# A two-block transformer forward pass on one core: one weight split ahead of a norm's last square, gated-attention scores ahead of their states, and row factors at the end on ScalarE and GpSimd

## The reference

```python
# first block, second norm
hffn = modulate(rmsnorm(x, g_norm2[l]), shift2, scale2)
a, u = jnp.split(jnp.einsum('bsd,df->bsf', hffn, w_ffn_in[l]), 2, axis=-1)

# second block, GLA in chunks of 64 tokens
att = jnp.where(causal, jnp.einsum('nbhtd,nbhsd->nbhts', q_in, k_in), 0.0)
o_intra = jnp.einsum('nbhts,nbhsv->nbhtv', att, vc)
def step(state, xs):
    qi, kd, vv, bl = xs
    o = jnp.einsum('bhtd,bhdv->bhtv', qi, state)
    state = state * jnp.exp(bl)[:, :, 0, :, None] + jnp.einsum('bhsd,bhsv->bhdv', kd, vv)
    return state, o

# the end
y = xf * lax.rsqrt(jnp.mean(xf * xf, axis=-1, keepdims=True) + EPS) * g
```

## Time and profile before

| | us |
|---|---|
| median of 3 runs | 1921.94 |
| lowest, highest run | 1920.91, 1922.42 |
| profiled execution, its own time | 1923.94 |
| its span | 1922.1 |
| PE busy | 1879.3 (98%) |
| DVE, ACT, POOL busy | 868.0, 687.2, 516.4 |

### The profile page before, as it was taken

One profiled execution on the slowest core, in us unless ns is written; L12 is line 12 of the kernel. 1 busy time (PEld: TensorE's weight loads), 2 busy tenths in 40 slices (PEclk: granted clock), 3 DMA queues, 4 the chain that ended last, 5 costly groups with the idle time before them and its releaser, 6 DMA issues.

```text
span 1922.1 us, 21539 instructions
## 1 busy us (share of the span) xinstructions
PE 1879.3 (98%) x8653; PEld 1463.2 (76%) x8653; DVE 868.0 (45%) x1352; ACT 687.2 (36%) x1021; POOL 516.4 (27%) x285
## 2 busy tenths in 40 slices
PE   7999999999999999989999999999999999999998
PEld 6777778878777777867888888777676778888886
DVE  6466542645261213334333333657477654423433
ACT  5555541223232323443221223425446432212223
POOL 4433334444353534410000000234345311100100
PEclk9999999999999999999999999999899999999999
DMA  9411223534443223324323322422122123222321
GB/s 302 144 46 65 66 66 132 175 121 153 132 141 100 66 88 110 102 74 118 114 82 95 108 80 77 113 88 84 58 72 73 46 99 104 93 88 89 108 88 44
DMA packets 182332, 192.47 MB, mean 100 GB/s; under 512 B 10155, under 2 KB 166065, under 8 KB 181977
## 3 DMA queue, kind: packets, MB, share of 16 engines
q1 hardware_dynamic: 179704, 180.84, 29.3%
q0 software_dynamic: 1104, 5.24, 1.0%
q10 hardware_dynamic: 1424, 5.00, 0.7%
HBM read 188.95 MB, written 4.72 MB: 101 GB/s over the span
## 4 chain that ended last, share of the span: by engine, by line
PE 87%; DVE 8%; ACT 2%; issue 2%; POOL 1%; DMA 0%; ACTq 0%; DVEq 0%; SPq 0%; POOLq 0%
PE bank L1465 23%; PE bank L1468 23%; PE bank L1466 23%; PE bank L1487 2%; PE bank L1486 2%; PE bank L1485 2%; PE bank L1561 2%; DVE left L1819 2%; PE bank L1495 1%; DVE ADA L1777 1%; PE bank L1531 1%; PE bank L1547 1%; PE bank L1511 1%; PE bank L1447 1%; PE bank L1448 1%
## 5 line engine op out<-in xcount | busy, mean ns | idle before, releaser
L2559 POOL TENSOR_TENSOR wl<-stg,wh 128x1024 fp32r<-128x1024 f32 x150 | 364.8, 2433 | 853.5 <-ACT wh L2200 853.1
L1465 PE MATMUL bank<-hH,wh 128*128 128x512 f32 x1264 | 522.6, 413 | 6.3 <-DVE hL L1933 6.0
L1468 PE MATMUL bank<-hH,wl 128*128 128x512 f32 x1264 | 502.4, 397 | 0.0
L1466 PE MATMUL bank<-hL,wh 128*128 128x512 f32 x1264 | 502.1, 397 | 0.0
L2200 ACT ACTIVATE wh<-stg 128x1024 fp32r<-128x1024 f32 (+2 forms) x292 | 298.3, 1024 | 283.6 <-PE bank L1468 202.8
L1465 PEld LDWEIGHTS bank<-hH,wh 128*128 128x128 f32 x1264 | 239.2, 189 | 78.4 <-issue 25.5
L1468 PEld LDWEIGHTS bank<-hH,wl 128*128 128x128 f32 x1264 | 238.9, 189 | 57.9
L1466 PEld LDWEIGHTS bank<-hL,wh 128*128 128x128 f32 x1264 | 239.8, 190 | 53.5 <-issue 2.9
L1759 DVE TENSOR_TENSOR wl<-stg,wh 128x1024 fp32r<-128x1024 f32 (+2 forms) x142 | 168.4, 1188 | 243.7 <-ACT wh L2200 243.2
L1465 PE MATMUL bank<-h2H,wh 128*128 128x512 f32 x352 | 140.6, 399 | 0.0
L1468 PE MATMUL bank<-h2H,wl 128*128 128x512 f32 x352 | 139.5, 396 | 0.0
(11 more groups left out here) (324 smaller groups left out, 2565.3 us busy)
## 6 DMA issues: line engine op xcount, KB each, us to landing
stg<-in_w_in SPq DMA_DIRECT2D x54, 1024.0 KB, 5.2
stg<-in_w_ffn_in SPq DMA_DIRECT2D x22, 1024.0 KB, 5.1
stg<-in_w_ada SPq DMA_DIRECT2D x16, 1024.0 KB, 5.2
stg<-in_w_ffn_gate SPq DMA_DIRECT2D x11, 1024.0 KB, 5.1
stg<-in_w_ffn_up SPq DMA_DIRECT2D x11, 1024.0 KB, 5.1
stg<-in_w_ffn_down SPq DMA_DIRECT2D x10, 1024.0 KB, 5.0
stg<-in_w_ada SPq DMA_DIRECT2D x16, 512.0 KB, 6.8
stg<-in_w_proj_ret SPq DMA_DIRECT2D x8, 1024.0 KB, 5.0
```

The costliest lines, as they stand in the source:

```text
L1465: T.matmul(ps, wh, xh, start=j["first"] and k == 0, stop=False)
L1466: T.matmul(ps, wh, xl, start=False, stop=False)
L1468: t = T.matmul(ps, wl, xh, start=False, stop=j["stop"] and last)
L2559: G.tensor_tensor(lo, src, hi, ALU.subtract).then_inc(s["w_lo_pool"], 1)
```

## The change

Three separate edits. First, the preparation of the FFN's third product stands in the last `out_job`, between the bank's release and the square, and no longer behind `a2`. Second, in the GLA the scores of a pair's first head stand ahead of the pair's states, three advances (before: one) lie between the states and `go`, and the scores of the second head stand right behind the first head's `go` step. Third, at the end DVE forms `fs/D + EPS` once per row behind the first half, ACT forms the factor alone as exp(-0.5 ln(...)) from the second half's sum, POOL scales the low half, and DVE the high half.

```diff
@@ out_job
             give(("gemm", n, 0))
+            if f == KT - 1:
+                p.prepare(p.ahead)
             sums("n2", f)
@@ norm2
         emit("a2")
-        p.prepare(p.ahead)
@@ gla
+        def scores(hd):
+            take("Z", ("gs", hd))
+            emit("gs", hd)
+            give(("gs", hd))
...
                 emit("kv", r, cc)
             yield
+            scores(2 * r)
+            yield
             emit("st", r)
             give(("kv", r, 0))
             give(("kv", r, 1))
-            yield
+            yield from rest(3)
             for hh in range(2):
                 hd = 2 * r + hh
-                take("Z", ("gs", hd))
-                emit("gs", hd)
-                give(("gs", hd))
-                yield
                 take("C", ("go", hd))
                 emit("go", hd)
                 yield
+                if hh == 0:
+                    scores(hd + 1)
                 emit("gsq", hd)
@@ sync, last_row
-                sp.wait_ge("a_end", 2 * i + 2)
+                sp.wait_ge("p_end", i + 1)
...
-                sp.wait_ge("v_end", 3 * i + 3)
+                sp.wait_ge("v_end", i + 1)
@@ vector, fin
                     V.tensor_tensor(dst, dst, GFB[:, 0:S], ALU.mult).then_inc(s["v_fin"], 1)
+                    V.tensor_scalar(fs[:, i:i + 1], fs[:, i:i + 1], 1.0 / D, EPS, ALU.mult, ALU.add).then_inc(s["v_fin"], 1)
@@ vector, last_row
-                ve.wait_ge("a_fin", 5 + i)
-                V.tensor_tensor(fd[:, i:i + 1], fs[:, i:i + 1], fs[:, 4 + i:5 + i], ALU.add).then_inc(s["v_end"], 1)
-                ve.wait_ge("a_end", 2 * i + 1)
-                V.reciprocal(fr[:, i:i + 1], fd[:, i:i + 1]).then_inc(s["v_end"], 1)
-                ve.wait_ge("v_end", 3 * i + 2)
+                ve.wait_ge("a_end", 2 * i + 2)
                 V.scalar_tensor_tensor(hi, hi, fr[:, i:i + 1], GFB[:, S:D], ALU.mult, ALU.mult).then_inc(s["v_end"], 1)
@@ scalar, fin
                     if c == 3:
-                        A_.preload_act_table(ACTF.Sqrt)
+                        A_.preload_act_table_set("natural_log_exp_and_others")
@@ scalar, last_row
-                lo = XT[:, i, 0:S]
-                ac.wait_ge("v_end", 3 * i + 1)
-                A_.activation(fd[:, i:i + 1], fd[:, i:i + 1], ACTF.Sqrt, bias=e6, scale=1.0 / D).then_inc(s["a_end"], 1)
-                ac.wait_ge("v_end", 3 * i + 2)
-                ac.wait_ge("v_fin", i + 1)
-                A_.activation(lo, lo, ACTF.Copy, scale=fr[:, i:i + 1]).then_inc(s["a_end"], 1)
+                ac.wait_ge("v_fin", 2 * i + 2)
+                ac.wait_ge("a_fin", 5 + i)
+                A_.activation(fd[:, i:i + 1], fs[:, 4 + i:5 + i], ACTF.Ln, bias=fs[:, i:i + 1], scale=1.0 / D).then_inc(s["a_end"], 1)
+                ac.wait_ge("a_end", 2 * i + 1)
+                A_.activation(fr[:, i:i + 1], fd[:, i:i + 1], ACTF.Exp, scale=-0.5).then_inc(s["a_end"], 1)
@@ gpsimd
+            def last_row(i):
+                lo = XT[:, i, 0:S]
+                po.wait_ge("a_end", 2 * i + 2)
+                G.tensor_scalar(lo, lo, fr[:, i:i + 1], None, ALU.mult).then_inc(s["p_end"], 1)
```

More of the change, by code:

```diff
@@ L1088 @@
 a_sq v_sq v_a2 v_n2 v_m1 v_x3 v_sc v_best a_gb v_gc a_gd v_gd a_ge p_gf a_gg p_gh a_gh p_gi
-kv_even v_st a_gsq a_gate p_gate v_mn p_al v_ag a_ae v_as av a_silu p_silu a_fin v_fin v_end a_end
+kv_even v_st a_gsq a_gate p_gate v_mn p_al v_ag a_ae v_as av a_silu p_silu a_fin v_fin v_end a_end p_end
 """.split()
@@ L2650, in qas @@
                     low("h4", pr, QA[:, pr, :])
+            def last_row(i):
+                lo = XT[:, i, 0:S]
+                po.wait_ge("a_end", 2 * i + 2)
+                G.tensor_scalar(lo, lo, fr[:, i:i + 1], None, ALU.mult).then_inc(s["p_end"], 1)
             mine = {"split": split, "n1": n1, "masks": masks_, "sbw": sbw, "ret_load": ret_load, "rot_sum": rot_sum, "rvv": rvv,
-                    "bias_first": bias_first, "bias_copy": bias_copy, "ffn_a": ffn_a, "gf": gf, "gh": gh, "gi": gi, "gn": gn, "lg": lg, "qas": qas}
+                    "bias_first": bias_first, "bias_copy": bias_copy, "ffn_a": ffn_a, "gf": gf, "gh": gh, "gi": gi, "gn": gn, "lg": lg, "qas": qas, "last_row": last_row}
             for name, *at in p.order:
```

## The result

The changed kernel takes 1918.65 us in the median of 15 runs (1916.75 to 1918.94), the kernel before 1921.79 us beside it (15 runs, 1920.91 to 1922.46): a ratio of 0.9981 with a 95% interval of 0.9973 to 0.9989, 3.1 us saved where 7.9 were forecast. The profiled execution of the changed kernel took 1918.94 us (span 1917.1), against 1923.94: 5.0 less. Lines of the code after the first edits stand 3 to 6 further down than before (L1465 is now L1471, L1933 is L1939, L1663 is L1669, L2077 is L2083).

A forecast was written before the change was run, and what follows sets the result against it. PE, busy 98% of the span, bounds the kernel, so time comes from its waits, low clock and the end's chain: -1.94 - 1.4 - 6.2 + 1.6 = -7.9, from 1923.9 to 1916.0, less 2.0 gives 1914.0 us; range 1911 to 1919.5.

The forecast's parts named there:

- the clock term of the second edit: GLA: the clock no longer falls, so 13.7 us of low clock at 0.455 save 6.2 us; bounds 0 and -6.8.
- First edit, -1.94: Second norm: the split moved into idle ACT and DVE time lets PE start at 857.90, not 859.84, saving 1.94 us.
- Rival D: Second norm: ACT takes the moved split no sooner and the square waits; up to 1.9 lost, 1915.9; inside the forecast's 0.62.
- I take no difference: Behind the second norm: the low clock for 4.4 us of PE's work stays as it was; bounds -2.0 and +1.0.
- rival B: Second norm: the clock does not fall there either, 2.0 less, 1912.0; chance 0.08.
- Second edit, waits, -1.4: GLA, first head: waits of 2.13 and 0.36 us give way to one of 1.1 ahead of the scores, saving 1.4 us.
- The other three heads: 0: GLA, remaining heads: the reordering changes nothing, taken as 0; bounds -0.5 to +1.5 for moved DVE waits.
- Rival A: GLA: the clock still falls as now, 1920.2, chance 0.16; for half as long, 1917, chance 0.10.
- the eight waits on L1495: Short PE waits of up to 1.0 us each that brought no clock fall, used as comparison for the new 1.1 us wait.
- the 2.0 taken off behind the sum: Whole kernel: the profiled execution lies 2.0 us above the timed median, so 1916.0 becomes 1914.0.
- Third edit, +1.6: Kernel end: POOL's scaling, taken as 1.0 us and meeting DVE's, delays the last DMA by 1.6 us; bounds -0.2 to +2.2.
- Rival C: GLA: the clock falls near 1351 and stays low far longer, making the kernel slower, 1926.9 at 27 us; chance 0.04.

The follow-up runs named there:

- before_r2: The unchanged kernel before, profiled a second time: profiled execution 1921.36 us, median of its timed runs 1922.19 us.
- norm: The kernel before with only the split moved ahead of the last square: 1922.37 us, ratio 0.9996 to the kernel before.
- norm_gla_l: The changed kernel without its POOL scaling at the end, and with the pair's first scores one advance later: 1913.50 us, ratio 0.9949 to the kernel before.

## Why the prediction was wrong

Forecast 1914.0, measured 1918.65, inside the range (1911 to 1919.5) but with 40% of the gain (3.1 of 7.9). The kernel is faster, since the interval ends below 1, but by 0.19%, just under the 0.2% that I had set as the bound. The step that failed is the clock term of the second edit, -6.2 us. It had the mechanism right (a wait, a fall, 0.455 us for each us of PE's work) and the size wrong twice over: an execution of before in the lower group, where its median lies, had 3.1 us to win there, not 6.2 (one profile, `before_r2`), and in the changed kernel's upper group, where its median lies, 1.5 of them go back by a new fall of 3.4 us (one profile). By steps:

- **First edit, -1.94: right.** The wait is 3.9 us (forecast 4.0), the split began within 0.1 us of the last tile's start, the square followed in its place, and with the clock at its full level the edit is worth 2.15. Rival D is out. "I take no difference" in the clock was right behind the norm itself (low for 4.4 us of PE's work in the first profiles of before and after; 3.4 to 6.0 in the others), and rival B did not come true. What it missed is that the edit alone gains nothing in the median; in both profiles of `norm` the clock's stretch 500 us later is the long one.
- **Second edit, waits, -1.4: near, by two errors that offset each other.** Rows show -1.1. "The other three heads: 0" was wrong: 0.84 us of a new wait, because the second head's square stands behind index copies on ACT. I had looked at PE's and DVE's queues there, not at ACT's. The wait of 0.5 on DVE's logits (0.51 in the prediction's bounds) went.
- **Second edit, clock, -6.2: this step failed.** "The new wait of 1.1 us is nearer to those of 1.0, so I take no fall": in the profile it did fall, for 3.4 us, in another execution it did not. Rival A in its shorter form had 0.10; this was closest to it. By the profile the term is -4.7. The comparison with the eight waits on L1495 took the wait's length alone and set aside that narrow matmuls surround this one, which the rival had named. Whether it is they that make the difference is not shown: the narrow ones alone did not bring a fall (`norm_gla_l`), and no run has such a wait among full ones.
- **The size of that step, and the 2.0 taken off behind the sum.** The 13.7 us were read from one execution, of the upper group. Its distance to the median, 2.0, is largely the same low clock: in the lower group the stretch is 6.8 us, 3.1 us cheaper. I counted it twice, once as regained and once as the offset. From the median, with 6.8 us: -1.94 - 1.4 - 3.1 + 1.6 = -4.8, that is 1917.1 with no fall at all, and the execution without one took 1916.92; with the fall of 3.4 us, 1.5 more, it is 1918.6, and the median is 1918.65. That they agree this closely is in part luck, since starts differ by up to 1.5 us. The changed kernel's profiled execution lies 0.3 above its median, not 2.0; this alone is 1.7 of the 4.65 missed. The other 2.9, counted between the two profiled executions, are: start 1.3, the clock 1.5, waits 0.3, the end and norm 0.1 each, less 0.3 left over.
- **Third edit, +1.6: right, +1.72 in the profile.** The operation on POOL takes 1.56 us where nothing is in its way and 2.12 beside DVE's scaling (forecast 1.0 and a meeting), the factor's Exp 0.20 and not 0.28. The upper bound for POOL, 1.29, was too low: both its ends came from other operations. So the forecast came out by luck: it had POOL's operation too short and let POOL wait for both of DVE's tiles, which it did only for one.
- **Rival C is out**: the low stretch became shorter.

The change's own balance: the first two edits are right, and placed one advance later the scores bring another 3.2 to 3.6 us; the third costs 1.7 and should go.

## What to carry to other kernels

Where the granted clock carries a term, take two profiled executions of the kernel before, and count how long it is low in each, before you call its distance to the median an offset. A wait that is cut from 2.1 to 1.1 us may still bring the clock down, so look at what else stands around it, and at the queue of every engine that a moved step passes (here ACT's index copies); full-width matmuls that nobody reads, just enough to fill the wait, test it in one run and may be kept. Before a job is handed to GpSimd at the end of a kernel, find the time of that very operation there (here 1.56 us against ScalarE's 0.72, read from no row beforehand) and ask which operands VectorE reads at that moment (0.56 more): the handover cost more than the factor's shorter chain gained.

## What was not expected of the hardware

- The trace's clock shows 1.00 until its first change. Over the profiled executions that first change lies between 17.3 and 20.7 us, and until then PE runs at the low rate (12 matmuls in 2 us against 20), worth up to 1.5 us between two executions of one kernel.
- The same wait of 1.05 us, in the same kernel, was followed by 3.4 us of low clock in one execution and by none in another; the same wait of 2.1 us by 13.7 and by 6.8. The profiles at hand and the granted clocks of the runs put the two groups of times down to this.
- POOL and DVE beside each other, one line's instructions in the changed kernel (ns min/median/max), both in SBUF:

```profile
L2658 POOL TENSOR_SCALAR XT<-XT,small x4: 1557/2121/2123, 1905.2 to 1912.4; 128x512 f32<-128x512 f32 x4
```

```profile
L2168 DVE SCALAR_TENSOR_TENSOR XT<-XT,small,GFB x4: 750/752/1179, 1905.1 to 1910.9; 128x512 f32<-128x512 f32 x4
```

POOL loses 0.56 us to DVE's 0.75, and one of DVE's tiles loses 0.43 to POOL. By the Trainium skill (SBUF — State Buffer, "SBUF: two separate sides") the port pair is locked by whichever starts first, for its whole instruction. The trace agrees that each holds the other up. It agrees less on "whole": DVE's last tile, which started while POOL worked on its third, was held for 0.43 us and not until POOL's end.
